# Tail of a two-layer language model on one Trainium2 core: the out-projection's first products between the samples' states, and seven unread products among narrow ones

## The reference

```python
def rwkv7_time_mix(h, shift, wkv0, ...):
    ...
    S_T, y = lax.scan(_wkv_step, wkv0, (r, decay, k, v, -kk, kk * a))
    y = (y - mean) * rsqrt(var + GN_EPS) * ln_w + ln_b
    y = y + sum(r * k * r_k) * v
    return (y * g) @ w_o, h[:, -1], S_T

hp = hp + y_p
hs = hs + y_s
hp = hp + sq_relu_mlp(rmsnorm(hp, norm_ffn[i]), ffn_w_up[i], ffn_w_down[i])
```

## Time and profile before

| | |
|---|---|
| median of three runs | 3323.68 us (3322.57 to 3330.06) |
| the profiled execution, its own time | 3323.09 us |
| its span in the profile | 3321.3 us |
| granted TensorE clock, mean of the span | 0.989 of full |
| TensorE busy | 3177.1 us, 96% |
| DVE, ScalarE, GpSimd busy | 1835.8, 1333.6, 1203.5 us |
| the tail and the out-projection's first half | about 2406 to 2541 us |

### The profile page before, as it was taken

The page is one execution under the profiler, slowest core; times in us unless marked ns, Lnnn a source line. Parts: engine busy times, 40 slices in busy tenths (PEclk is TensorE's granted clock), DMA queues, the critical chain, the costliest instruction groups (busy, mean ns, idle before and its releaser), DMA issues.

```text
span 3321.3 us, 69887 instructions
## 1 busy us (share of the span) xinstructions
PE 3177.1 (96%) x25744; PEld 2884.9 (87%) x25744; DVE 1835.8 (55%) x3139; ACT 1333.6 (40%) x2785; POOL 1203.5 (36%) x842
## 2 busy tenths in 40 slices
PE   8999999998999999999999999999989999999998
PEld 6688887687999999997899878787868899999998
DVE  3466664216544477766303477778733644458885
ACT  2244444412544533322213355565521354443332
POOL 0000000010766777721222222332222276677771
PEclk9999999999999999999999999999989999999999
DMA  3122224400544544422223201100151154454442
GB/s 112 43 79 72 61 76 153 170 13 20 164 156 156 177 143 143 143 78 80 78 70 122 73 19 35 39 27 30 37 190 32 41 169 156 156 185 142 137 139 76
DMA packets 305364, 331.44 MB, mean 100 GB/s; under 512 B 54350, under 2 KB 286721, under 8 KB 305058
## 3 DMA queue, kind: packets, MB, share of 16 engines
q1 hardware_dynamic: 299138, 309.17, 29.4%
q0 software_dynamic: 6048, 19.73, 1.9%
HBM read 232.57 MB, written 116.69 MB: 105 GB/s over the span
## 4 chain that ended last, share of the span: by engine, by line
PE 69%; DVE 9%; PEld 6%; issue 5%; POOL 5%; ACT 3%; SPq 2%; DMA 1%; DVEq 0%; PEldq 0%; ACTq 0%; POOLq 0%
PE bank L644 66%; PEld bank L644 6%; PE bank L652 4%; POOL wloA L2050 2%; POOL arena L2050 1%; DVE arena L3566 1%; SPq L1737 1%; DVE hT L3637 1%; POOL wloS L2050 1%; SPq L1678 1%; DVE x_mix L3517 0%; SPq L1732 0%; DVE arena L3025 0%; POOL table L2050 0%; DMA arena<-in_rwkv_w_o 0%
## 5 line engine op out<-in xcount | busy, mean ns | idle before, releaser
L644 PE MATMUL bank<-arena 128*128 128x268 f32 (+18 forms) x7294 | 942.2, 318 | 51.0 <-DVE hT L3637 12.9
L644 PEld LDWEIGHTS bank<-arena 128*128 128x128 f32 (+7 forms) x7294 | 732.5, 167 | 234.7 <-issue 34.5
L2268 ACT COPY arena<-bank 128x512 f32<-128x512 f32 (+15 forms) x523 | 232.9, 484 | 620.8 <-PE bank L644 413.5
L2050 POOL TENSOR_TENSOR arena<-arena 128x512 f32<-128x512 f32 x120 | 164.4, 1370 | 639.4 <-PE bank L644 412.4
L2491 ACT ACTIVATE whiS<-arena 128x512 fp32r<-128x512 f32 x180 | 113.0, 628 | 407.9 <-POOL arena L2050 394.6
L2050 POOL TENSOR_TENSOR wloA<-arena,whiA 128x512 fp32r<-128x512 f32 x180 | 262.0, 1470 | 1.4 <-ACT whiA L2488 1.4
L2050 POOL TENSOR_TENSOR wloS<-arena,whiS 128x512 fp32r<-128x512 f32 x180 | 239.1, 1343 | 49.1 <-ACT whiS L2491 49.1
L3432 DVE TENSOR_TENSOR hT<-hT,bank 128x536 f32<-128x536 f32 x280 | 197.3, 706 | 79.7 <-PE bank L644 79.2
L652 PE MATMUL bank<-table,arena 128*128 128x128 f32 (+5 forms) x1422 | 181.6, 269 | 30.6 <-DVE arena L3145 13.0
L644 PE MATMUL bank<-hiT,whiS 128*128 128x268 f32 x768 | 199.1, 288 | 7.5 <-DVE loT L3270 3.8
L3275 DVE TENSOR_TENSOR arena<-std,bank 128x268 f32<-128x268 f32 x192 | 80.3, 432 | 217.7 <-PE bank L644 204.5
(11 more groups left out here) (322 smaller groups left out, 8557.8 us busy)
## 6 DMA issues: line engine op xcount, KB each, us to landing
u_scratch<-arena SPq DMA_DIRECT2D x480, 134.0 KB, 1.9
arena<-in_ffn_w_up SPq DMA_DIRECT2D x64, 512.0 KB, 4.1
arena<-u_scratch SPq DMA_DIRECT2D x56, 536.0 KB, 4.9
arena<-in_ffn_w_down SPq DMA_DIRECT2D x112, 256.0 KB, 4.2
arena<-u_scratch SPq DMA_DIRECT2D x56, 402.0 KB, 5.7
arena<-past_scratch SPq DMA_DIRECT2D x32, 640.0 KB, 6.9
past_scratch<-in_cache_kv_latent SPq DMA_DIRECT2D x128, 128.0 KB, 2.4
past_scratch<-in_cache_k_rope SPq DMA_DIRECT2D x128, 32.0 KB, 2.2
```

Of the source, the lines that this page charges most:

```text
L644: return pe.matmul(out, lhsT, rhs, start=first, stop=last, skip_group_check=group)
L2050: return pool.tensor_tensor(out, a, b, op)
L2268: lane.do(act.copy(dst, b if view is None else view(b)), ring.drained)
```

## The change

On TensorE the first product with `w_o` moves ahead of the tail's solving: `tail_between(n)`, called behind each of the 16 steps of the first two quarters, has the inverse's products in step 0, the outputs in step 1, `change(n - 2)` from step 2 on, and `turn_new(n - 3)` from step 3 to 11. Only step 3 waits for `tok_s`. `gates(8)` goes right behind "seen", `gates(7)` behind six of eight `turn_state`. In "seen", each of samples 0 to 6 gets one `keep_busy(rv)` in its middle. DVE's `centre`, `variances` and scaling of the tail move into steps 2 to 4 of its adds.

For this the places are moved: the tail's masked products leave `hT` (`RR_tail`, `NR_tail`), `FT` and the gates too, and z of chunk 7 goes straight to `zT` and not through DRAM. SP loads `w_o` and the first quarter's hidden values earlier, then three chunks of z, `wo2[7]`, keys by sample, four chunks of z (`z_rest`, waited for in step 7), and behind the outputs (`y_b`) all values by sample.

```diff
-                        if q == 0 and also is not None:
-                            also(k)
+                        if q < 2 and also is not None:
+                            also(q * KT + k)
...
-            gates(7, P)
...
             for n in range(DB):
+                if n == 6:
+                    gates(7, P)
                 pe.wait_ge(st_in[n // 2], 64)
                 turn_state(states[n])
...
                 for ct in range(8):
                     for rows in halves_of:
                         ends.append(mm(seen_by(ct, n + 1)[rows], states[n][rows, turned_at_ct(ct), :], ar[rows, ct, :, seqs[n + 1]], True, True))
+                    if ct == 3 and n < DB - 1:
+                        keep_busy(rv)
             ra.done(ends[7])
             ra.done(ends[15])
             mark["tail_seen"] = ra.filled.n
+            gates(c, w)
+            mark["tail_gates"] = rv.filled.n
             turn_z(7, P, Y[1])
...
+            def tail_between(n):
+                if n == 0:
+                    solved()
+                if n == 1:
+                    outputs()
+                if n == 3:
+                    pe.wait_ge(tok_s, 4 * DB * 16)
+                if 2 <= n <= DB + 2:
+                    change(n - 2)
+                if 3 <= n <= DB + 3:
+                    turn_new(n - 3)
+                if n == KT - 1:
+                    pe.wait_ge(z_rest, 16)
+                if n == DB + 3:
                     mark["states_out"] = ra.filled.n
...
-            v_in[0].wait(sp, 4)
-            by_sample(values_4, DS, vt[0])
+            y_b.wait(sp, 7)
+            sp.wait_ge(s_done, 1)
             load(wo2_23, w[:, 2:4, :], wo2_t)
-            sp.wait_ge(a_drained, mark["tail_seen"])
             load(wo2_456, w[:, 4:7, :], wo2_t)
+            z_out.wait(sp, 6)
+            hidden = h_d.rearrange("p (k t) -> p k t", k=KT)
+            load(hT[:, :, 0:TS], hidden[:, :, 0:TS], hid_t)
             gc_b.wait(sp, 8)
             load(wo2_01, w[:, 0:2, :], wo2_t)
+            sp.wait_ge(a_drained, mark["tail_seen"])
+            load(zT[:, :, 0:3 * P], z_d[:, :, 0:3 * P], Tally(z_back))
+            sp.wait_ge(v_drained, mark["tail_gates"])
+            load(wo2[7], w[:, 7, :], wo2_t)
             zt_b.wait(sp, 7)
             by_sample(keys_4, 0, Btok)
             by_sample(keys_4, DS, Ktok)
-            z_out.wait(sp, 7)
-            load(zT[:, :, 0:8 * P], z_d[:, :, :], Tally(z_back))
-            sp.wait_ge(a_drained, mark["tail_solved"])
+            load(zT[:, :, 3 * P:7 * P], z_d[:, :, 3 * P:7 * P], Tally(z_rest))
+            v_in[0].wait(sp, 4)
+            y_b.wait(sp, 8)
+            by_sample(values_4, DS, vt[0])
             by_sample(values_4, 0, SA_tail)
-            y_b.wait(sp, 8)
...
+            def two_quarters():
+                for n in range(2 * KT):
+                    if n in (0, KT):
+                        dve.wait_ge((hid_s, hid_rest)[n // KT], 16)
+                    s, l = QUARTERS[n // KT]
+                    add_hidden(n % KT, l * TH + s * TS, TS)
+                    if 2 <= n <= DB + 2:
+                        new_state(n - 2)
```

More of the change, by code:

```diff
@@ L1577, in _ @@
             v_in[0].wait(pe, 4)
-            rv.wait_drained(3)
+            rv.wait_drained(6)
             ra.wait_drained(2)
@@ L1581, in _, with solved, outputs @@
                 tail_sums(half, 0, lambda out, h: None)
[L1582 to L1593, removed]
+            def solved():
+                pe.wait_ge(xt_tail_s, 1)
+                for half in range(2):
+                    ra.wait_drained(1)
+                    b = ra.bank()
+                    for j in range(8):
+                        h = 8 * half + j
+                        ins = mm(b[0:w, j * RN:(j + 1) * RN], XT_tail[:, h * w:(h + 1) * w], P1_tail[0:w, h * RN:(h + 1) * RN], True, True)
+                    ra.done(ins)
+            def outputs():
+                for half in range(2):
+                    ra.wait_drained(1)
+                    tail_sums(half, 1, lambda out, h: mm(out, RR_tail[0:w, h * w:(h + 1) * w], SA_tail[0:w, h * RN:(h + 1) * RN], False, False, True))
             def change(n):
@@ L1641, in out_product_1 @@
                 product(rv, lambda j: wo2[j][:, k * P:(k + 1) * P], lambda j: zT[:, j, at:at + w], KT, w=w)
[L1643 removed]
+            added(1, out_product_1, tail_turned, tail_between)
             mark["tiles"] = {}
@@ L3296, in out_12 @@
                     with_product(g, order, W_3, s, f.us["12", s], eu[s])
-                if first_quarter is None:
+                if two_quarters is None:
                     adds(0, *range(KT))
+                    adds(1, *range(KT))
                 else:
-                    for k in range(KT):
-                        first_quarter(k)
-                adds(1, *range(KT))
+                    two_quarters()
                 adds(2, 0, 1)
@@ L3883, in _ @@
                 take(gates_tail[:, at:at + n], TAIL, n)
-            y_b.wait(dve, 8)
-            centre(8, TAIL, Y[0])
             sn_t = Tally(snew_s)
@@ L3907, in gated_tail @@
                 signal(dve.tensor_tensor(Y[0][0:TAIL, :], Y[0][0:TAIL, :], gates_tail, ALU.mult), z_b)
[L3909 to L3927 removed]
+            def two_quarters():
[6 more added lines that the diff above has]
+                        new_state(n - 2)
+                    if n == 2:
+                        y_b.wait(dve, 8)
+                        centre(8, TAIL, Y[0])
+                    if n == 3:
+                        variances(8, TAIL)
+                    if n == 4:
+                        scale_outputs(8, TAIL, Y[0])
+                    if n == KT + 1:
+                        gated_tail()
+            feed(1, two_quarters)
             dve.wait_ge(fin_w, 16)
```

71 lines of the change are left out of this document (21 added, 50 removed).

## The result

The changed kernel takes **3335.79 us** (median of 7 runs, 3328.42 to 3339.65) against 3323.68 us (7 runs, 3318.66 to 3330.06): the ratio is 1.0034 with a 95% interval of 1.0022 to 1.0045. It is slower by 11 us by the ratio and by 12 by the medians, outside the range of 3313 to 3331.

A forecast was written before the change was run, and what follows sets the result against it. TensorE, busy 96% of the span, was taken as the bound. Terms brought the third quarter's start 3.1 us earlier: 3323.09 - 3.1 + 0.6 = 3320.6 us, own range 3315 to 3325, 8-in-10 range 3313 to 3331.

The forecast's parts named there:

- Step 2: Narrow products and work behind them: 9.0 us saved if the seven unread products hold the clock, 4.9 in the narrow ones.
- Step 3: Price of seven unread products among the narrow ones: 0.55 us each, 3.9 us in all (3.0 to 4.7).
- the clock falls in the narrow products all the same: Rival: section at half clock takes 21.8 instead of 13.2 us; 3329.3 us (3327 to 3333), slower; chance 0.25.
- Step 5: Gates of chunk 7 moved behind six states' transposes: cost nothing, as TensorE waits there for the last states either way.
- Step 1: Ahead of the first product on `w_o`: idle waits of 11.50 and 2.03 us removed, 13.5 us saved.
- Step 6: Behind the narrow products: new wait for z and the last `w_o` piece, 1.7 us (0 to 4).
- Step 7: Two products behind the outputs: new wait for copies by sample, 3.6 us (2 to 11.5), plus 1.0 for the clock.
- Step 4: Four products now precede the new state's last transposes: 14.5 us added there, no cost by itself at the third quarter.
- A and B: A, end of a new state's last transposes: 2511.04 to 2513.2 us; B, third quarter's first product: 2541.03 to 2537.9.
- the roundings are no obstacle: Rival: ScalarE and GpSimd finish before TensorE reaches the third quarter, 12.3 us earlier: 3311.4 us; chance 0.09.
- The copies by sample land late: Rival: the wait behind the outputs is as long as the old 11.5 us, 8 us more: 3328.5 us; chance 0.08.
- The rule on transposes: Skill's rule: transposes don't count as work for the clock, so it falls ahead of the section; chance 0.03 of 0.25.

The follow-up runs named there:

- kernel 2: The changed kernel with two unread products in each of the eight samples, 16 in all instead of seven: 3334.83 us, ratio to before 1.0038.
- kernel 9: As the fastest kernel (copies and squares ahead of roundings, values on GpSimd's queue), but with 32 unread products, four per sample: 3326.84 us, ratio 1.0013.
- kernel 10: As the fastest kernel (copies and squares ahead, values on GpSimd's queue), with seven unread products in one block ahead of the narrow ones: 3309.61 us, ratio 0.9957.
- kernel 4: The changed kernel with the gates of chunk 7 back ahead of the samples' states: 3337.14 us, ratio to before 1.0041.
- kernel 6: The changed kernel without unread products, ScalarE's copies, squares and deviations ahead of its roundings, eight value copies on GpSimd's queue: 3307.04 us, ratio 0.9957.
- kernel 3: The changed kernel with ScalarE's copies of the tail's z ahead of the seven roundings: 3329.31 us, ratio to before 1.0018.
- Kernel 1: The changed kernel without its seven unread products: 3323.48 us, ratio to before 0.9997.
- kernel 12: Repeat of kernel 6, nothing changed: 3306.60 us, ratio to before 0.9949.

## Why the prediction was wrong

- **Step 2, the clock, failed.** It counted 9.0 us on the sentence "if the seven products hold the clock". They did not: 0.50 from the middle of the third sample. Of the 4.9 us for the narrow products 0.5 came (80 of the 256 at full clock, where before took 12.3 us for all), and the eight transposes behind took 1.97 us as before; only the terms of 0.8 and 1.8 us came. Kernels 2, 9 and 10 show the same: seven did not do it, spread or in a block, sixteen did for 14 us, 32 for the section. What was taken as evidence, other parts of the program with such products at 1.00, had products of 64 and 128 columns between them (before, 2390 to 2406 us); that it was these that held the clock there is not shown.
- **Step 3, the price, failed in size.** It put 0.55 us on a product, with bounds of 0.43 and 0.67: 3.9 us. Measured are 0.73 at full and 1.23 at half clock, 7.1 us in all. Its lower bound is nearly the block's 0.46: that bound holds where like stands beside like. The row of 0.67 us in the chunks was nearer and should have been taken as the middle.
- **Section, steps 2 and 3 together.** Forecast 13.2 and 1.7 us for the gates, 14.9 us to the transposes of z; measured 24.40. The 9.5 us more are 4.4 of narrow products at half clock (176 x 0.025), 3.2 of unread products (7.1 for 3.9) and 1.9 of the gates at half clock (3.6 for 1.7). The rival, "the clock falls in the narrow products all the same", had 21.8 us and, with the gates at half clock (3.3), 25.1. It was given 0.25 and was what happened. Its condition, "0.50 in the first samples", is seen, though two and a half samples escaped. That its 3329.3 us is what the profiled execution took (3329.35) is luck: it had the tail 5.6 us longer, the tail was 8.2 us longer, and that execution was 2.5 us ahead for other reasons; the median lies outside its 3327 to 3333.
- **Step 5, the gates moved at "nothing", failed.** TensorE reached the section 2420.39 - 2405.68 = 14.71 us behind the offset, before 2419.82 - 2408.15 = 11.67: 3.0 us later. Its idle time in that stretch was 2.83 us in before (1.17 ahead of the gates, 1.66 ahead of the last states) and came in one piece of 3.33 now; with it the clock fell, and the gates ran at half: 3.62 us for six records, 1.89 at full clock in kernel 4. The transposes on both sides of them lost the rest. Kernel 4 reached its section 11.6 us behind the offset, so step 5 is what cost the 3.0; but its section was 4.0 us longer, and nothing was left of it in the end.
- **Step 1 was right,** the 11.50 and 2.03 us went. **Step 6:** 0.54 us against 1.7 (0 to 4): the load landed 10.4 us behind the last narrow product and not 8.3, but gates, transposes and sums took 9.9 us of it, in part at half clock, and not 6.6. **Step 7:** 3.02 against 3.6, and kernel 6 shows SP's issuing as its cause. The clock then fell as step 7 had it, at more than its 1.0 us: the next 48 records took 6.54 us against 4.86. **Step 4:** from the first product on `w_o` to A it took 72.5 us, forecast 71.9.
- **A and B.** A was 2524.1 against 2513.2, and with the lead of 2.5 us taken out 13.4 us late: 3.0 of step 5, 9.5 of the section, 0.9 of the rest. From A to the product that is B 22.6 us were measured and 22.9 forecast, with the idle stretch of 7.53 against 7.5; the 1.8 us of half clock that the forecast adds ahead of B came behind it, as 1.4 (32 records in 8.87 us against 7.49). So this part was right, in mechanism and size. So "the roundings are no obstacle" fell, by the profile and by kernel 3. "The copies by sample land late" fell as well.
- **What stays open.** The medians differ by 12.1 us and the profiles by 6.3, or by 8.2 in the tail alone. Kernel 1, too, is 12.3 us away by medians, 9.1 by profiled executions and 8.5 from the offset to B. The sections account for 6.3 to 8.5 us in three pairs of kernels. Why the median of the change lies some 4 us above that is open: the mean granted clock is 0.987 in its runs of 3329.35 and of 3339.65 us alike, and one execution of seven has a trace. Parts that no edit touches move single executions by as much: kernel 6 and kernel 12, the same kernel, took 3307.04 and 3311.03 us in their profiles, and kernel 12's was 4.5 us behind already at the offset.
- **The rule on transposes.** The prediction gave it 0.03. In the changed kernel the clock was at 1.00 in 2409 to 2413, where TensorE had 15 transposes and else was idle, and at 0.50 behind the 3.33 us. In kernel 4 it stayed at 1.00 from 2413 to 2420, with 27 transposes, nine records of 32 columns and 2.97 us of idle time. No run has transposes alone, so this is not settled; the loss does not need it.

## What to carry to other kernels

A product that nobody reads is paid in full where TensorE is the bound, and more than its columns where it stands among narrow ones (0.73 us against 0.46 in a block). It can only pay if the clock gives back more than that; work out first what the stretch loses at half clock (here 6.4 us for 256 records). Where a kernel waits behind a section, look for small things in the way, such as two copies and a sum of squares behind seven roundings (10.8 us by medians) or 16 small transfers on one queue (3.0 to 5.7 us): together they were worth more than the unread products cost, 7 to 12 us.

## What the runs showed of the hardware that was not expected

- The clock fell with TensorE busy 14.20 of 14.20 us on products of 8 and of 256 columns, and with 16 unread products after 14 us of the same mixture at 1.00. The Trainium skill ("TensorE: Matmul & The Clock Gate", Part 1) names idle time as what brings the clock to its low level; the trace disagrees for products this narrow, which are busy by the profile and still at 0.50.
- An unread product of 256 columns takes 0.46 us among its like, 0.73 among products of 8 columns on 64 rows, both at full clock, and 1.23 us there at half.
- Where the clock falls differs from one execution to the next of one kernel: the section of kernel 6 took 18.17 us in one profile and 16.19 in the other (kernel 12), with the fall 3.0 and 5.5 us behind its start.
